# Input projection and state-space heads as one program over halves of the tokens, in three fp32r passes

## The reference, cut to what matters

```
x = rmsnorm(h) * norm1_g                     # 2112 tokens (2048 prompt + 64 sample) x 1024
proj = x @ w_in                              # 1024 x 2304
u, zr = proj[:, :512], proj[:, 512:]         # 4 column tiles of u, 14 of zr
# state-space heads, 32 groups of 16 channels, 64 complex states each
bu = u_group @ Bb                            # per group
h_t = A * h_{t-1} + bu_t                     # complex, diagonal, over the tokens
y = gelu(Re(C h) + D u)
y = y * sigmoid(y @ w_glu + b_glu)
# zr feeds the RWKV heads (delta_rule); both feed w_out, FFN and embedding (out_ffn_embed)
```

## Time and profile before

| | us |
|---|---|
| median of three runs (3848.49 to 3854.6) | 3851.16 |
| the profiled execution, its own time | 3846.97 |
| its span, first to last instruction | 3845.1 |
| `project_in`, to the last product | 541 |
| `state_space`, from there to the first instruction of `delta_rule` | 444 |
| mean granted PE clock | 0.935 |

### The profile page before, as it was taken

One profiled execution on the slowest core, in us unless ns is written; L12 is line 12 of the kernel. 1 busy time (PEld: TensorE's weight loads), 2 busy tenths in 40 slices (PEclk: granted clock), 3 DMA queues, 4 the chain that ended last, 5 costly groups with the idle time before them and its releaser, 6 DMA issues.

```text
span 3845.1 us, 76669 instructions
## 1 busy us (share of the span) xinstructions
PE 3444.8 (90%) x32800; PEld 3107.6 (81%) x32800; DVE 2036.7 (53%) x3764; ACT 1100.5 (29%) x2151; POOL 441.6 (11%) x427
## 2 busy tenths in 40 slices
PE   7999984089699989987799999999999999999998
PEld 4666653066588888876799999999999999999998
DVE  2111127951466666653455555665655566665565
ACT  1001021001344444442322222452222245222224
POOL 0000000000343333320300000210000031000001
PEclk9999996559799999997899999999999999999999
DMA  5010011000211111011532222432332243232223
GB/s 202 27 39 26 26 46 13 0 2 23 70 28 28 28 28 37 28 13 55 155 106 72 75 70 69 140 105 84 100 101 71 70 141 105 66 102 76 66 76 115
DMA packets 371665, 257.80 MB, mean 67 GB/s; under 512 B 29584, under 2 KB 361872, under 8 KB 371344
## 3 DMA queue, kind: packets, MB, share of 16 engines
q1 hardware_dynamic: 371360, 253.23, 21.6%
HBM read 217.99 MB, written 34.03 MB: 66 GB/s over the span
## 4 chain that ended last, share of the span: by engine, by line
PE 47%; DVE 3%; ACT 1%; issue 1%; DMA 1%; POOL 0%; SPq 0%; POOLq 0%; DVEq 0%; ACTq 0%
PE oe_pg L892 13%; PE oe_pv L892 13%; PE oe_pd L920 13%; PE oe_pg L953 4%; PE oe_pd L940 3%; PE oe_pv L960 1%; DVE oe_w_lo L702 1%; DVE oe_rms L733 0%; ACT oe_w_hi L553 0%; DVE oe_x L718 0%; DMA oe_raw<-in_w_out 0%; DMA oe_raw<-in_w_ple 0%; POOL oe_ys_lo L501 0%; POOL oe_acc L519 0%; PE oe_pn L881 0%
## 5 line engine op out<-in xcount | busy, mean ns | idle before, releaser
L244 PE MATMUL in_pp<-in_xn,in_w 128*128 (+1 forms) x1728 | 513.9, 460 | 3.7 <-DVE in_xn L200 3.7
L244 PEld LDWEIGHTS in_pp<-in_xn,in_w 128*128 128x128 f32 x1728 | 329.1, 191 | 188.1 <-issue 5.5
L702 DVE TENSOR_TENSOR oe_w_lo<-oe_raw,oe_w_hi 128x1024 fp32r<-128x1024 f32 (+1 forms) x294 | 381.5, 1308 | 116.3 <-ACT oe_w_hi L553 90.8
L709 DVE TENSOR_TENSOR oe_h<-oe_pd,oe_h 128x352 f32<-128x352 f32 x576 | 292.3, 522 | 188.3 <-PE oe_pd L920 140.7
L920 PE MATMUL oe_pd<-oe_f_hi,oe_w_hi 128*128 128x352 f32 x1056 | 342.9, 325 | 8.7 <-DVE oe_h L709 8.2
L892 PE MATMUL oe_pg<-oe_xs_hi,oe_w_hi 128*128 128x352 f32 x1056 | 342.4, 324 | 6.1 <-DVE oe_xs_lo L723 6.0
L892 PE MATMUL oe_pg<-oe_xs_lo,oe_w_hi 128*128 128x352 f32 x1056 | 340.6, 323 | 0.0
L920 PE MATMUL oe_pd<-oe_f_lo,oe_w_hi 128*128 128x352 f32 x1056 | 340.5, 322 | 0.0
L920 PE MATMUL oe_pd<-oe_f_hi,oe_w_lo 128*128 128x352 f32 x1056 | 340.5, 322 | 0.0
L892 PE MATMUL oe_pg<-oe_xs_hi,oe_w_lo 128*128 128x352 f32 x1056 | 340.4, 322 | 0.0
L892 PE MATMUL oe_pv<-oe_xs_lo,oe_w_hi 128*128 128x352 f32 x1056 | 339.9, 322 | 0.0
(11 more groups left out here) (423 smaller groups left out, 6933.7 us busy)
## 6 DMA issues: line engine op xcount, KB each, us to landing
oe_raw<-in_w_gate SPq DMA_DIRECT2D x66, 512.0 KB, 4.1
oe_raw<-in_w_val SPq DMA_DIRECT2D x66, 512.0 KB, 4.1
oe_raw<-in_w_down SPq DMA_DIRECT2D x66, 512.0 KB, 3.8
oe_raw<-in_w_out SPq DMA_DIRECT2D x48, 512.0 KB, 3.8
oe_raw<-in_w_pg SPq DMA_DIRECT2D x48, 512.0 KB, 3.8
scratch_zr<-in_zout SPq DMA_DIRECT2D x12, 1232.0 KB, 4.7
rw_Z<-scratch_zr SPq DMA_DIRECT2D x15, 903.0 KB, 5.4
in_w<-in_w_in SPq DMA_DIRECT2D x6, 1536.0 KB, 16.1
```

The lines of the kernel that those rows point to most:

```text
L244: mm = pe.matmul(pp[m % back][:, 0:TW], w[:, k, m * P:(m + 1) * P], xn[:, k, cols(n)], start=(k == 0), stop=(k == KD - 1))
L702: dve.tensor_tensor(w_view(kind, lo), w_view(kind, raw[i % 2]), w_view(kind, hi).bitcast(F32), ALU.subtract).then_inc(w_lo, 1)
L709: dve.tensor_tensor(hm, pd[sums[key] % 3][:, 0:TW], hm, ALU.add).then_inc(h_ready, 1)
```

## The change

`project_in` and `state_space` become one function, `front`, in one block. `front_order` writes down one order of units that PE, ACT and SP follow: the tokens in two halves of 1024 (the samples ride with the first), each half three token tiles of 320 to 368 (`FT`).

- Unit `("z", n, m)`: one column tile of `zr` for one token tile, 24 fp32r products (8 contraction steps x 3 passes). ACT alone copies out, and each unit is stored by itself.
- Unit `("u", lot, s, c)`: the tokens `s, s+8, s+16, ...` are the stationary operand and two column tiles of `w_in` (256 columns) the moving one, so `u` comes out as rows of blocks and the transposes of stage (1) at L2221 fall away. 24 products each, 34 units.
- Units `"U"`, `"K"`, `"R"`, `"b"` are stages (1) to (4), placed between the z units; the scan of stage (5) starts after the last `b` of the second half, with 30 z units still to come on PE.
- `w_in` is no longer held: its column tiles pass through a ring of four, once for each half (`RING`, 36 tiles in 72 half tiles). A half tile is loaded by SP, rounded by ACT, and POOL subtracts for the rest. The normalised tokens are split by ACT and DVE. DVE sums the squares with adds in place of one reduction.
- `Ks` goes to DRAM, and `Tm` is built from there after the last z unit, in the memory of the ring. The diagonal D is added to `Ks` (16 columns a group) and not to `Tm`.
- The scan joins real and imaginary parts: six instructions a step in place of eight.
- Of the outputs, the samples come first, then the two halves. The gate is as before.

```diff
-def project_in(nc, ins, scratch, u):
...
-def state_space(nc, ins, outs, u, y):
...
+HT, TS = SEQ // 2, DB * DS
+XW = HT + TS
+FT = ((0, 352), (352, 368), (720, 368), (0, 352), (352, 352), (704, 320))
+RING = [(h, kind, m) for h in range(2)
+        for kind, ms in (("z", range(4)), ("u", range(KU)), ("z", range(4, ZT))) for m in ms]
+RING_AT = {w: i for i, w in enumerate(RING)}
+LOTS = {0: (0, P), 1: (P, P), 2: (NBL, NBS)}
+def front_order():
+    for h in range(2):
+        ns = range(3 * h, 3 * h + 3)
+        for n in ns:
+            for m in range(4):
+                yield ("z", n, m)
+                if n == 5:
+                    yield ("R", 2 * m)
+                    yield ("R", 2 * m + 1)
+        for c in range(2):
+            if h == 0:
+                yield ("u", 2, 0, c)
+            for s in range(L):
+                yield ("u", h, s, c)
+            if h == 1 and c == 0:
+                for f in range(4):
+                    yield ("U", 1, f)
+        if h == 1:
+            for f in range(4, 8):
+                yield ("U", 1, f)
+            for x in range(2):
+                for j in range(NJ):
+                    yield ("b", x, j)
+        turn = 0
+        for m in range(4, 10 if h == 0 else ZT):
+            for n in ns:
+                yield ("z", n, m)
+                if h:
+                    continue
+                if m == 4:
+                    for f in range(3 * (n % 3), min(3 * (n % 3) + 3, 8)):
+                        yield ("U", 0, f)
+                if m == 5:
+                    for f in range(3 * (n % 3), min(3 * (n % 3) + 3, 8)):
+                        yield ("U", 2, f)
+                if m >= 7 and turn < NG_ // 4:
+                    yield ("K", turn)
+                    turn += 1
+        if h == 0:
+            for n in ns:
+                for m in range(10, ZT):
+                    yield ("z", n, m)
...
+                def weights(i):
+
+                    h, kind, m = RING[i // 2]
+                    if i >= 3:
+                        sp.wait_ge(w_lo_ready, i - 2)
+                    c = m * P if kind == "u" else (KU + m) * P
+                    ks = slice(4 * (i % 2), 4 * (i % 2) + 4)
+                    sp.dma_start(raw[:, i % 3], ins["w_in"][ks, :, c:c + P].rearrange("k p c -> p k c")).then_inc(w_in[i % 3], 16)
...
+                    if unit == ("U", 0, 7):
+                        sp.wait_ge(side_mm, side_done("U", 0, 7))
+                        sp.wait_ge(side_out, side_done("u", 2, 0, 1))
+                        for s in range(L):
+                            sp.dma_start(u_rows[0][0:NBS].rearrange("p (g s c) -> p g s c", s=L, c=GC)[:, :, s, :],
+                                         smp[s:s + L * (NBS - 1) + 1:L, :].rearrange("p (g c) -> p g c", c=GC)).then_inc(smp_moved, 16)
...
+                store(*before)
+
+                sp.wait_ge(tm_zero, 1)
+                sp.wait_ge(ks_stored, 16)
+                for s in range(L):
+                    sp.dma_start(Tm[s * GC:(s + 1) * GC, :, s * GC:P], ks_mem[:, :, 0:P - s * GC]).then_inc(tm_in, 16)
...
+                for i in range(2 * len(RING)):
+                    s, ks = i // 2 % 4, slice(4 * (i % 2), 4 * (i % 2) + 4)
+                    pool.wait_ge(w_hi_ready, i + 1)
+                    pool.tensor_tensor(w_lo[:, s, ks], raw[:, i % 3], w_hi[:, s, ks].bitcast(F32), ALU.subtract).then_inc(w_lo_ready, 1)
+                wait_last_use(pool, len(RING) - 4)
+                wait_last_use(pool, len(RING) - 3)
+                pool.memset(Tm, 0.0).then_inc(tm_zero, 1)
...
+                def weights(j):
+                    if j >= 4:
+                        wait_last_use(act, j - 4)
+                    for i in (2 * j, 2 * j + 1):
+                        act.wait_ge(w_in[i % 3], 16 * (i // 3 + 1))
+                        ks = slice(4 * (i % 2), 4 * (i % 2) + 4)
+                        act.copy(w_hi[:, j % 4, ks], raw[:, i % 3]).then_inc(w_hi_ready, 1)
...
+                def norm(n):
+                    w = FT[n][1]
+                    q = sq[:, :, 0:w]
+                    dve.wait_ge(sq_ready, n + 1)
+                    tt(q[:, 0:4], q[:, 0:4], q[:, 4:8], ALU.add)
+                    tt(q[:, 0:2], q[:, 0:2], q[:, 2:4], ALU.add)
+                    if n:
+                        dve.wait_ge(ms_ready, n)
+                    dve.tensor_tensor(ssum[:, 0:w], q[:, 0], q[:, 1], ALU.add).then_inc(ssum_ready, 1)
+                    dve.wait_ge(rms_ready, n + 1)
+                    link(dve.reciprocal(rms[:, 0:w], rms[:, 0:w]))
...
+                    for i in range(2):
+                        ks = slice(4 * i, 4 * i + 4)
+                        dve.wait_ge(x_hi, 2 * n + i + 1)
+                        dve.tensor_tensor(xs[:, 1, ks, cols(n)], q[:, ks], xs[:, 0, ks, cols(n)].bitcast(F32), ALU.subtract).then_inc(x_lo, 1)
...
+                def add_product(X, a, B, t):
+                    shape = list(X.shape)
+                    both = a[0].unsqueeze(1).to_broadcast(shape)
+                    tt(t[:, 0], B, both, ALU.mult)
+                    tt(t[:, 1, 0], B[:, 1], a[1], ALU.mult)
+                    tt(t[:, 1, 1], B[:, 0], a[1], ALU.mult)
+                    tt(X, X, t[:, 0], ALU.add)
+                    tt(X[:, 0], X[:, 0], t[:, 1, 0], ALU.subtract)
+                    tt(X[:, 1], X[:, 1], t[:, 1, 1], ALU.add)
...
+                dve.wait_ge(side_out, side_done("b", 1, NJ - 1))
+                link(dve.memset(H[:, :, :, 0:1], 0.0))
+                a8 = [bcast(Qp[:, x, 1, :], BI) for x in range(2)]
                 for i in range(1, BI):
...
+                def three(l, r):
+                    return [(l[0], r[0]), (l[0], r[1]), (l[1], r[0])]
+                def mean_square(n):
+                    pe.wait_ge(ssum_ready, n + 1)
+                    if n:
+                        pe.wait_ge(rms_ready, n)
+                    pe.matmul(pn[:, 0:FT[n][1]], ones[:], ssum[:, 0:FT[n][1]], start=True, stop=True).then_inc(ms_ready, 1)
+                def z_unit(n, m):
+                    i, w, r = z_at[n, m], FT[n][1], RING_AT[n // 3, "z", m]
+                    pe.wait_ge(w_lo_ready, 2 * r + 2)
+                    if m == 0:
+                        pe.wait_ge(x_lo, 2 * n + 2)
+                    if i >= 4:
+                        pe.wait_ge(z_out, i - 3)
+                    out = pp[i % 4][:, 0:w]
+                    for k in range(KD):
+                        lot = three([ring[:, r % 4, a, k, :] for a in range(2)], [xs[:, a, k, cols(n)] for a in range(2)])
+                        for p, (lhsT, rhs) in enumerate(lot):
+                            mm = pe.matmul(out, lhsT, rhs, start=(k == 0 and p == 0), stop=(k == KD - 1 and p == 2))
+                    mm.then_inc(z_mm, 1)
+                def u_unit(out, lot, s_, c):
+                    pe.wait_ge(w_lo_ready, 2 * RING_AT[int(lot == 1), "u", 2 * c + 1] + 2)
+                    slot = RING_AT[int(lot == 1), "u", 2 * c] % 4
+                    tokens, n = (slice(HT, XW), TS) if lot == 2 else (slice(s_, s_ + L * (P - 1) + 1, L), P)
+                    for k in range(KD):
+                        lot3 = three([xs[:, a, k, tokens] for a in range(2)], [ring[:, slot:slot + 2, a, k, :] for a in range(2)])
+                        for p, (lhsT, rhs) in enumerate(lot3):
+                            mm = pe.matmul(out[0:n, 0:2 * P], lhsT, rhs, start=(k == 0 and p == 0), stop=(k == KD - 1 and p == 2))
+                    return mm
...
```

More of the change, by code:

```diff
@@ new lines, in front @@
+def front(nc, ins, outs, scratch, y):
+    order = list(front_order())
+    z_at, side_at, first, last = {}, {}, {}, {}
+    for q, u in enumerate(order):
+        if u[0] == "z":
+            z_at[u[1:]] = len(z_at)
+            used = [RING_AT[u[1] // 3, "z", u[2]]]
+        else:
+            side_at[u] = len(side_at)
+            used = [RING_AT[int(u[1] == 1), "u", 2 * u[3] + i] for i in range(2)] if u[0] == "u" else []
+        for i in used:
+            first.setdefault(i, q)
+            last[i] = q
+    NZ, NSIDE = len(z_at), len(side_at)
+    with ExitStack() as ctx:
+        e = Env(nc, ctx, "fr")
+        raw = e.sb("raw", [P, 3, KD // 2, P])
+        zout = e.sb("zout", [P, 3, 368])
+        U = e.sb("U", [P, NG_, NBT])
+        H = e.sb("H", [P, 2, NJ, NBL + 1])
+        CA = e.sb("CA", [P, 2, NJ, L + 1, GC])
+        BC = e.sb("BC", [P, 4, NJ, GC])
+        Bb = e.sb("Bb", [P, 2, NJ, GC])
@@ L2031, in _ @@
-                for j in range(NJ):
-                    act.wait_ge(b_mm, 2 * j + 1)
-                    src = bk[(2 * j) % 8]
-                    act.copy(H[0][:, j, 1:], src[:, 0:NBL])
-                    act.copy(HS[0][:, j, :], src[:, NBL:NBT]).then_inc(b_act, 1)
-                for lot, (b0, n, _) in enumerate(LOTS):
+                act.wait_ge(const_ready, 2)
+                square(0)
+                weights(0)
+                root(0)
+                x_high(0)
+                weights(1)
@@ L2153, in _ @@
```

(11 more changed lines are left out.)

746 lines of the change are left out of this document (368 added, 378 removed).

## The result

The changed kernel takes 3761.19 us (median of four runs, 3759.42 to 3764.12) beside 3849.82 us of the kernel before (four runs of the same comparison): ratio 0.9768, 95% interval 0.9752 to 0.9785. It is faster by 88.6 us; forecast were 208 us. The profiled execution has a span of 3757.6 us.

What follows compares the result with a forecast made beforehand. Bounds: PE's fp32 projection products up to 541 us, then DVE's unhidden scan. Last z unit at 536, plus 17.5, 53, 67, 39 and 64 gives 777 us in place of 985: 208 us less, 3643 us; range 3590 to 3700 us.

Steps and rivals of the forecast that it cites:

- the price of a product of u: Products with tokens eight apart as stationary operand: 0.13 us each, near the transposes, 816 of them, 106 us.
- upper bound of 144 us: All u products if bound by loading, from fp32 output products at 0.176 us a record.
- rival 2: u products bound by loading, 0.159 to 0.176 us each: 24 to 38 us more, 3667 to 3681 us; chance 0.13.
- The first product: Head of the kernel: parameter loads, square and token splits put PE's first product at 30 us.
- The waits: PE's stalls before the last z unit: sums of squares, samples' DMAs, hand-overs and 3 us of lower clock, 33 us.
- The z products: 2016 fp32r products of 352 columns on the mean at 0.159 us: 321 us.
- `Tm`'s gap: Behind the last z unit, PE idles 17.5 us for the band matrix's copy, store and DMAs.
- the samples and the first half at the lower clock: After the `Tm` gap the clock stays near 0.5: samples 53 us, first half 67 us.
- the scan under its cover: DVE's scan ends before the first half's outputs start, covered by 112 us of z, `Tm` and samples; PE never waits.
- Rival 1: Clock comes back in the samples or first half: first half 39 us, total 3594 to 3615 us; chance 0.16.
- Rival 3: Feed by DMA, ACT and POOL sets the pace where four tiles change: 3665 to 3710 us; chance 0.13.
- Rivals 4 and 5: 4: fp32r at 256 columns runs at fp32's pace, 3888 us, chance 0.05; 5: scan uncovered, 3764 us, chance 0.02.

Runs made afterwards that it cites:

- the second kernel of pitches: Changed kernel plus ten further lots of 64 unread products behind z unit (0,12), run once; side-by-side moving tokens at 352 columns took 0.160 us a product.
- the filling products: 20 unread fp32 products between the samples' short transposes and first half's outputs, added to the kernel whose `Tm` gap 36 such products filled: 3727.24 us.

## Why the prediction was wrong

The step that failed is the price of a product of u, as the prediction put it: stage (1) has such tokens, a transpose of them has a pitch of 0.116 us, "so a load alone is no longer than that and the step is not dear". The row is right and the inference is not: a transpose of tokens eight apart costs 0.110 us, a product with them as stationary operand 0.237 to 0.245 us in fp32 and fp32r. The term of 106 us measured 98.5 us in the first half and 46.5 + 46.4 us in the second, 191 us. Its upper bound of 144 us, and the 38 us more of rival 2, came from rows with neighbouring columns and were too low for the same reason. Rival 2 named the cause, loading, with too small a price. The prediction's own sign against it, a pitch of u above 0.16 us, came.

The 85 us of u are most of the 124 us by which the last z unit was late. The rest is in the smaller terms. The first product came at 33.2 us (30 forecast). The waits, put at 29.5 us without the 3 us for the clock, were 48 us: the five sums after the first 28.3 us, of them 7.4 us each at sums 4 and 5, where ACT's square waited for the tile's load; the turns of the second half 9.9 us, where ACT's copies are queued behind its work on weights; the samples' DMAs 6.5 us; block kernel and `b` 3.6 us.

The z products, 321 us forecast, were busy for 340.1 us. The pitch itself was right: 0.155 us in the 112 us without a wait, at 341 columns on the mean, and 0.160 us at 352 columns in the second kernel of pitches. But behind the four longest of these waits (6.5 to 9.2 us) the granted clock was 0.50 for 3.5 to 5.8 us, here behind sum 4 with 8 products in place of 14:

```profile
356.00:358.00 2.00, 2.00 (x8) 2.00 (x7) 1.19 (x1) 1.58 (x3) 0.63 (x1) 0.50 0.56 174
358.00:360.00 2.00, 2.00 (x14) 2.00 (x13) 1.97 (x2) 0.00 (x0) 1.90 (x2) 1.00 0.05 14
```

As an estimate, half of the 19 us at 0.50, that is some 10 of the 19 us; where the rest lies is not shown. The sum had set down 3 us for the clock, so the parts come to 85 + 3 + 19 + 16 = 123 us of the 124.

What held: z's pitch where nothing waits, `Tm`'s gap (14.5 us for 17.5), the samples and the first half at the lower clock (51 and 65 us for 53 and 67), the second half at the full one (38 for 39), and the scan under its cover: no product waits for the states. For the first half the time was right and the reason only in part: with the gap filled or gone it still ran at 0.50, behind the samples' short transposes, which the prediction had named as a thing that might lift the clock. DVE needed 170 us for the scan beside POOL, where 152 and 9 to 24 us were put down. Rival 1 did not occur by itself; what it would have taken is shown by the filling products. Rival 3 did not show here: PE waits for no weight tile in the kernel after, nor with u fast; only where the layout, the later sums and the early band matrix stand together did one wait of 2.4 us come. Rivals 4 and 5 fell with u at 0.242 us and the wait that never came. With the one price right, 0.121 us, the forecast would have been 3636 us; the kernel with neighbouring tokens takes 3674 us. The other 38 us are the first product, the waits and z, the clock behind the waits among them.

## What to carry to other kernels

A price taken from another kind of instruction has to be tried on the instruction itself: the transposes showed that a transpose keeps its pitch with a step, not that a product does. Where a layout gives a step to an operand, price the step at the operand that has it, and look for an order of the data that pays it once, on an engine with time to spare (here stationary tokens two apart cost no more than neighbours). And at a change of stage look at what runs directly ahead of a long stretch of PE: 14.5 us of idle PE and 2 us of tiny transposes each cost 23 to 26 us of clock.

## What the runs showed that I had not expected

- A step of 4 to 8 fp32r tokens in the stationary operand: 0.229 to 0.241 us a product at 256 columns, in place of 0.120; in the moving one 0.233 us too (step 4); in a transpose 0.110 us in place of 0.109.
- The clock went to the lower level after 2 us of 8x8 transposes and stayed there through 63 us of busy output products; 20 fp32 products of 256 columns brought it back, and so did 32 transposes of 128x128. It fell as well in a lot of fp32r products of 128 columns with step 8, with PE busy throughout.
- ACT's and DVE's splits of 1408 elements went from 1.37 and 1.62 us to 2.98 and 2.92 us where they read one token in eight.
